# adaLN chunks of a diffusion trunk step: four column strips of the array instead of one, folded by the product that turns them

## The reference

```
mod = (silu(cond) @ w_ada + b_ada)          # cond: one row for context, one for latent; w_ada: 1024 x 6144
sh1, sc1, gt1, sh2, sc2, gt2 = split(mod, 6)
h = rms_norm(x, g_mix) * (1 + sc1) + sh1;  p = h @ w_in
# three mixers on p: attention (8 heads), chunked gated linear attention (GLA), RWKV-7, forward and backward
merged = sum over mixers of sigmoid(gate) * (mixer @ w_po)
x = x + gt1 * (merged @ w_out)
x = x + gt2 * ((silu(u) * v) @ w_ffn_out)   # (u, v) from (rms_norm(x, g_ffn) * (1 + sc2) + sh2) @ w_ffn_in
```

## Time and profile before

| what | value |
|---|---|
| median of three runs | 2113.26 us |
| the profiled execution: own time | 2109.75 us |
| the profiled execution: span | 2107.8 us |
| TensorE busy | 1912.7 us (91%) |
| DVE, ACT busy | 1011.0 us, 817.6 us |
| adaLN matmuls (L606), busy | 175.5 us |
| mean granted TensorE clock | 0.968 |

### The profile page before, as it was taken

One profiled execution on the slowest core, in us unless ns is written; L12 is line 12 of the kernel. 1 busy time (PEld: TensorE's weight loads), 2 busy tenths in 40 slices (PEclk: granted clock), 3 DMA queues, 4 the chain that ended last, 5 costly groups with the idle time before them and its releaser, 6 DMA issues.

```text
span 2107.8 us, 38529 instructions
## 1 busy us (share of the span) xinstructions
PE 1912.7 (91%) x16691; PEld 1552.8 (74%) x16691; DVE 1011.0 (48%) x1755; ACT 817.6 (39%) x1340; POOL 147.6 (7%) x325
## 2 busy tenths in 40 slices
PE   6899899986889898999989999999678989899998
PEld 3799455644566598999989975456356759899998
DVE  0326435856754354343333444177767445433432
ACT  2433545343433335333243345253534343533321
POOL 2000000005220000000000000000232200000000
PEclk9999999998999999999999999999889999999999
DMA  6533324220212443443433432333010034344342
GB/s 229 181 122 111 101 67 149 93 74 2 93 52 82 154 120 81 134 126 100 131 125 103 136 99 83 123 128 101 25 42 23 3 90 133 84 130 131 103 122 85
DMA packets 267934, 214.46 MB, mean 102 GB/s; under 512 B 7225, under 2 KB 259544, under 8 KB 267512
## 3 DMA queue, kind: packets, MB, share of 16 engines
q1 hardware_dynamic: 264816, 204.41, 31.5%
q0 software_dynamic: 2736, 7.54, 1.1%
q10 hardware_dynamic: 216, 0.06, 0.0%
HBM read 209.10 MB, written 2.88 MB: 101 GB/s over the span
## 4 chain that ended last, share of the span: by engine, by line
PE 76%; DVE 10%; ACT 9%; issue 3%; DMA 1%; PEldq 1%; ACTq 0%; PEld 0%; POOL 0%; DVEq 0%; SPq 0%; POOLq 0%
PE bank L555 11%; PE bank L557 11%; PE bank L556 11%; PE bank L611 9%; PE bank L606 7%; PE bank L1166 3%; PE bank L1167 3%; PE bank L1168 3%; PE bank L974 3%; PE bank L617 2%; PE bank L515 2%; PE bank L814 2%; ACT h L1348 1%; PE bank L916 1%; DVE scr_rounded L1782 1%
## 5 line engine op out<-in xcount | busy, mean ns | idle before, releaser
L557 PE MATMUL bank<-scr_rounded 128*128 128x384 f32 (+1 forms) x1312 | 444.1, 338 | 0.0
L555 PE MATMUL bank<-scr_rounded 128*128 128x384 f32 x672 | 232.5, 346 | 37.1 <-DVE scr_rounded L1787 35.6
L557 PEld LDWEIGHTS bank<-scr_rounded 128*128 128x128 f32 (+1 forms) x1312 | 249.7, 190 | 1.0
L611 PE MATMUL bank<-h,ring 128*128 128x384 f32 x640 | 233.8, 509 | 13.5 <-ACT gtmp L1331 8.0
L556 PE MATMUL bank<-scr_rounded 128*128 128x384 f32 x672 | 229.9, 342 | 0.0
L1782 DVE TENSOR_TENSOR scr_rounded<-ring,scr_rounded 128x2048 fp32r<-128x2048 f32 (+1 forms) x64 | 136.0, 2126 | 191.0 <-ACT scr_rounded L1339 190.2
L555 PE MATMUL bank<-scr_rounded,gate_rounded 128*128 128x384 f32 (+1 forms) x640 | 214.8, 336 | 4.4 <-DVE scr_rounded L1782 4.4
L556 PE MATMUL bank<-scr_rounded,gate_rounded 128*128 128x384 f32 (+1 forms) x640 | 214.4, 335 | 0.0
L611 PEld LDWEIGHTS bank<-h,ring 128*128 128x128 f32 x640 | 118.2, 194 | 96.0 <-issue 26.8
L606 PE MATMUL bank<-ring,scond 128*2 128x256 f32 x768 | 175.5, 381 | 9.0 <-DVEq L350 5.0
L1782 DVE TENSOR_TENSOR scr_rounded<-ring,gate_rounded 128x2048 fp32r<-128x2048 f32 (+3 forms) x64 | 130.1, 2033 | 106.1 <-ACT gate_rounded L1339 105.6
(11 more groups left out here) (383 smaller groups left out, 3236.5 us busy)
## 6 DMA issues: line engine op xcount, KB each, us to landing
ring<-in_w_in_dram SPq DMA_DIRECT2D x56, 1024.0 KB, 5.1
ring<-in_w_ada_dram SPq DMA_DIRECT2D x48, 1024.0 KB, 5.3
ring<-in_w_ffn_in_dram SPq DMA_DIRECT2D x88, 512.0 KB, 5.0
ring<-in_w_ffn_out_dram SPq DMA_DIRECT2D x32, 704.0 KB, 4.6
ring<-in_w_out_dram SPq DMA_DIRECT2D x8, 1024.0 KB, 5.2
ring<-in_w_po_a_dram SPq DMA_DIRECT2D x4, 1024.0 KB, 6.9
ring<-in_w_po_b_dram SPq DMA_DIRECT2D x4, 1024.0 KB, 5.9
ring<-in_w_po_c_dram SPq DMA_DIRECT2D x4, 1024.0 KB, 5.1
```

The costliest lines, as they stand in the source:

```text
L555: pe.matmul(o, w_hi[:, k, :], right[0][k], start=k == 0, stop=False)
L557: ins = pe.matmul(o, w_lo[:, k, :], right[0][k], start=False, stop=k == nk - 1)
L611: ins = pe.matmul(b[:, 0:T], w[:, k, 128 * (j % 2):128 * (j % 2) + 128], h[:, k, :], start=k == 0, stop=k == KD - 1)
```

## The change

The 8 matmuls of a chunk go to four column strips of the array: k = 0 to 3 open partitions 0, 32, 64 and 96 of the bank, k = 4 to 7 add to them. So there are four partial pairs of rows. ACT copies all 128 partitions of the bank. In place of the transposes two products with a constant `fold` (1 where the partition modulo 32 is the column) add the four and turn them. The fill banks are cleared once at the start, since unwritten partitions are now read. A chunk is one step of a fill and no longer two, so the numbers of steps are spread anew: both `fill(4)` at the start become `fill(2)`; in attention every third pair gets 3 steps; in GLA's loop steps alternate 1 and 2; layer 0's row of `FILLS` sums to 48 and no longer 56.

```
-        modrow = sb("modrow", [2, 2, 256])
+        modrow = sb("modrow", [128, 2, 256])
+    put("fold", p[:, None] % 32 == np.arange(2)[None, :])
...
-        FILLS = ((4, 6, 2, 1, 1, 1, 1, 0, 1, 1, 1, 2, 2, 2, 1, 1, 3, 2, 2, 1, 1, 3, 2, 2, 1, ...
+        FILLS = ((4, 6, 2, 1, 1, 1, 1, 0, 1, 1, 1, 1, 1, 2, 1, 1, 2, 2, 1, 1, 1, 2, 2, 1, 1, ...
...
                 for i in range(2):
-                    ins = turn(b[:, 2 * i:2 * i + 2], modrow[0:2, j % 2, 128 * i:128 * i + 128])
+                    ins = pe.matmul(b[:, 2 * i:2 * i + 2], modrow[:, j % 2, 128 * i:128 * i + 128], K("fold"), start=True, stop=True)
...
                         for k in range(KD):
-                            ins = pe.matmul(b[0:2, 0:256], scond[:, :, k], w[:, k, :], start=k == 0, stop=k == KD - 1)
-                            if k == 3:
-                                yield
+                            strip = 32 * (k % 4)
+                            ins = pe.matmul(b[strip:strip + 2, 0:256], scond[:, :, k], w[:, k, :], start=k < 4, stop=k >= 4)
...
-            fill(4)
+            pe.wait_ge(S["strips_clear"], 1)
+            fill(2)
...
-                    fill(2)
+                    fill(3 if pair % 3 == 0 else 2)
...
                 for n in range(2 * LEVELS):
-                    fill(2)
+                    fill(2 if n % 2 else 1)
...
-                        A(modrow[0:2, j % 2, :], bank(*t)[0:2, 0:256], ACT.Copy).then_inc(*empties(*t))
+                        A(modrow[:, j % 2, :], bank(*t)[:, 0:256], ACT.Copy).then_inc(*empties(*t))
...
+            dve.memset(banks[6][:, :], 0.0).then_inc(*step())
+            dve.memset(banks[7][:, :], 0.0).then_inc(*tells("strips_clear"))
```

More of the change, by code:

```diff
@@ L20 @@
 ROPE_THETA, GRID_W = 10000.0, 64
-_COLS = [("ident", 128), ("ones", 128), ("blocks", 128), ("eps", 4), ("dup", 256), ("duprot", 256), ("rot", 128),
+_COLS = [("ident", 128), ("ones", 128), ("blocks", 128), ("eps", 4), ("fold", 2), ("dup", 256), ("duprot", 256), ("rot", 128),
          ("cos", 256), ("sin", 256), ("upper", LEVELS * 128), ("lower", LEVELS * 128),
@@ L271, in step_kernel @@
         S = {n: sem(n) for n in (
-            "zeroed", "squares", "rstd", "normed",
+            "zeroed", "strips_clear", "squares", "rstd", "normed",
             "att_squares", "att_rstd", "att_normed", "att_keys", "att_queries", "att_max", "att_probs",
@@ L336, in counting @@
             return step, tells, empties, lambda: last, before
-        PER.update(zeroed=0, squares=8, rstd=2, padded=2, ffo_half=8, normed=16, h_hi=24, h_lo=24, src_hi=1, src_lo=1, mg_hi=8, mg_lo=8, ff_hi=NF, ff_lo=NF,
+        PER.update(zeroed=0, strips_clear=0, squares=8, rstd=2, padded=2, ffo_half=8, normed=16, h_hi=24, h_lo=24, src_hi=1, src_lo=1, mg_hi=8, mg_lo=8, ff_hi=NF, ff_lo=NF,
                    att_squares=1, att_rstd=5, att_normed=5, att_keys=1, att_queries=1, att_max=24, att_probs=24,
@@ L353, in barrier @@
                     eng.wait_ge(phase[other], l * NPHASE + k + 1)
-        FILLS = ((4, 6, 2, 1, 1, 1, 1, 0, 1, 1, 1, 2, 2, 2, 1, 1, 3, 2, 2, 1, 1, 3, 2, 2, 1, 1, 1, 1, 1, 1, 1, 2, 2, 2),
+        FILLS = ((4, 6, 2, 1, 1, 1, 1, 0, 1, 1, 1, 1, 1, 2, 1, 1, 2, 2, 1, 1, 1, 2, 2, 1, 1, 1, 1, 1, 1, 1, 1, 2, 1, 1),
                  (4, 6, 2, 1, 1, 1, 1, 0, 1, 1, 1, 1, 1, 1, 1, 1, 2, 1, 1, 1, 1, 2, 1, 1, 1, 1, 1, 1, 1, 1, 1, 1, 1, 1))
```

## The result

The changed kernel takes 2098.8 us (median of 4 runs, 2096.8 to 2104.0), the kernel before 2116.1 in the same session: a ratio of 0.9925, 95% interval 0.9907 to 0.9942. It is faster by 0.75%: the direction was forecast, the size was not. The forecast of 2040 was 59 us too low, and 2098.8 lies outside its range (2013 to 2067).

What follows compares the result with a forecast made beforehand. TensorE was taken to bound the kernel (76% of the chain). Gains of 15 (start) + 2 x 13 (attention) + 2 x 7.6 (GLA) + 15 (RWKV, layer 0) = 71 us gave 2038.5, stated as 2040; range 2013 to 2067.

Steps and rivals of the forecast that it cites:

- Chunk and fold: On TensorE, a chunk takes 0.97 us and its fold 0.35; together 1.32 instead of 3.75.
- Rivals B: Two strips run at a time, so a chunk is 0.87 us longer: 2061 us in all; chance 0.13.
- E (serial): Strips' records are issued one after another; nothing is saved and each fold adds 0.14 us: 2120 us; chance 0.04.
- the prediction's signs of being wrong: Wrong if a chunk takes 1.8 us or more, TensorE never waits for loads in attention, or GLA's loop still takes 64.
- The start: Up to the first projection: weight loads, not the row of chunks, end last; first projection at 49.5 us, gain 15.
- Attention: Each layer's attention takes 104 us, a gain of 13, with 7.2 us of new waits for gate weight loads.
- one late fold or so adds 1: In attention, besides the waits for gate loads, a late fold or so costs 1 us per layer.
- GLA: Each layer gains 7.6 us; DVE bounds the loop, which takes 57 us and ends at 421.3 instead of 428.9.
- Its first `gla_z` comes from ACT and DVE and does not move: In GLA, the first `gla_z`, made by ACT and DVE, keeps its old time, with the loop's blocks counted from 364.08.
- RWKV of layer 0: Its 8 chunks give a gain of 15 us (12.6 to 17.8), if the new 1.32 us are all exposed.
- So a chunk costs (28.3 - 5.2) / 8 = 2.9 to 3.5 of its 3.75: From the 28.3 us between RWKV's two layers, each chunk costs 2.9 to 3.5 of its 3.75 us.
- Rival C: Load waits at the start, in attention and in GLA exceed the count: gain 43 us, 2069 in all; chance 0.10.

Runs made afterwards that it cites:

- experiment 9: Only the first of the four strips multiplied (a quarter of each sum), against the kernel with strips and the old step counts (2075.5 us): 2077.9 us.
- experiment 7: 8 idle matmuls put into two TensorE waits (GLA's scaled keys, attention's late gate load), against the kernel with strips and the old step counts (2075.5 us): 2069.8 us.
- experiment 5: Changed kernel with three step numbers altered: attention's three steps every second pair, five steps ahead of GLA's scaled keys, GLA's loop counts swapped: 2079.6 us.
- experiment 4: Changed kernel with adaLN's weights not loaded but for one chunk; each chunk multiplies whatever weights its neighbour in the plan has in the ring: 2070.8 us.
- the kernel of 1: Strips and fold as in the changed kernel, but the step counts of before and a chunk in two steps again: 2075.5 us.
- experiment 3: Changed kernel with five steps instead of six ahead of the wait for GLA's scaled keys: 2109.2 us.
- Experiment 8: Each chunk's strips multiplied a second time into columns nobody reads, against the kernel with strips and the old step counts (2075.5 us): 2082.2 us.
- experiment 10: RWKV layer 0's 8 chunks moved to the end of GLA's plan, against strips with old step counts and reordered attention (2068.9 us): 2074.4 us.

## Why the prediction was wrong, step by step

**Chunk and fold: right.** 0.97 and 0.36 at the high clock. Rivals B (two strips at a time) and E (serial) are out by these rows and by experiment 9. None of the prediction's signs of being wrong came either: a chunk takes 1.05 at the high clock, attention waits 5.5 for loads, and GLA's loop takes 59.2 and 56.9 instead of 64. They watch the terms that were priced; the loss lay in what the sum took as unchanged.

**The start, 15 forecast, 9.9 measured.** The step that failed is the clock, which the sum put at its high level for everything behind the first two chunks; "the loads are late instead" holds only with it. In the changed kernel the start is as long without adaLN's loads (54.8), and what ends last is TensorE's own row of chunks, at the low clock. Here are a stretch of the changed kernel, and then of the kernel of experiment 7, whose start has the same chunks at the same places; the ACT rows are the split of the first projection weights.

```profile
27.31 1.89 PE L608 MATMUL bank<-ring,scond 128*2 128x256 f32 x16 [2.46 <-ACT modrow L1319]
29.12 1.01 PE L591 MATMUL bank<-cst,modrow 128*128 128x2 f32 x4
30.00 7.02 PE L541 MATMUL bank<-mg,cst 128*128 128x384 f32 x16
...
45.27 1.89 PE L608 MATMUL bank<-ring,scond 128*2 128x256 f32 x16
...
47.56 1.90 ACT L1340 ACTIVATE scr_rounded<-ring 128x2048 fp32r<-128x2048 f32 x1
```

The kernel of experiment 7:

```profile
26.63 1.05 PE L611 MATMUL bank<-ring,scond 128*2 128x256 f32 x16 [2.46 <-ACT modrow L1331]
27.60 0.61 PE L591 MATMUL bank<-cst,modrow 128*128 128x2 f32 x4
28.07 5.41 PE L541 MATMUL bank<-mg,cst 128*128 128x384 f32 x16
...
42.70 1.91 ACT L1352 ACTIVATE scr_rounded<-ring 128x2048 fp32r<-128x2048 f32 x1 [1.40 <-DMA ring<-in_w_in_dram]
...
49.93 0.66 PE L556 MATMUL bank<-scr_rounded 128*128 128x384 f32 x1 [7.91 <-DVE scr_rounded L1800]
```

After the same wait of 2.46 us the one is at the low clock (granted 0.50 from 27 to 31) and the other is not (1.00 from 26.6 to 42). In the latter the split waits for its load and starts at 42.70, where 42.3 was forecast, and the first projection comes at 49.93, where 49.5 was forecast. So the mechanism of the start holds at the high clock, and 5 us of the miss were the clock. Experiment 7's edit does not touch the start. The kernels of this text whose start has these same chunks and loads reach the first projection between 49.9 and 54.8, and why one start keeps the high clock and another does not stays open.

**Attention, 13 forecast, 3.9 measured in each layer.** The waits for loads came nearly as counted (5.5 against 7.2). What failed is "one late fold or so adds 1". I followed only the ring's slots and not the two fill banks: at three places the new counts put a chunk right behind a gate's last step and a fold, one bank is the fold's, and the other is the gate's until ACT's sigmoid has emptied it. That is 6.2 us in each layer, and 3.4 to 3.5 more by the low clock on unchanged work. Experiments 5 and 4 take the two waits away one at a time, and attention falls to 101.6 to 104.5 and to 103.1.

**GLA, 7.6 forecast, 4.5 lost in layer 0 and 2.4 won in layer 1.** The loop was nearly right: with the old spread it ends after 58 us (57 forecast), and DVE holds it. What failed is "Its first `gla_z` comes from ACT and DVE and does not move". In the changed kernel the first block product came 40.3 us after the stage's first matmul in layer 0, before 32.2 (364.12 less 331.93). Ahead of it TensorE waits for DVE's scaled keys, before too (the prediction calls it a wait for ACT). The transposes behind that wait, before:

```profile
357.44 1.09 PE L515 MATMUL bank<-cst,scr 128*128 128x128 f32 x8 [2.42 <-DVE scr L1965]
```

The setup after the change:

```profile
318.08 3.58 PE L759 MATMUL bank<-arena,lora 32*128 32x384 f32 x8 [0.75 <-DVEq L351]
321.58 2.93 PE L769 MATMUL bank<-arena 64*128 64x128 f32 x24
324.44 6.58 PE L617 MATMUL bank<-arena,ring 128*128 128x384 f32 x16
...
340.50 1.91 PE L608 MATMUL bank<-ring,scond 128*2 128x256 f32 x32 [0.42 <-DVE mg L1773]
345.27 0.58 PE L591 MATMUL bank<-cst,modrow 128*128 128x2 f32 x4 [2.86 <-ACT modrow L1319]
349.57 1.97 PE L516 MATMUL bank<-cst,scr 128*128 128x128 f32 x8 [3.72 <-DVE scr L1968]
351.47 3.24 PE L801 MATMUL bank<-gate,scr 128*64 128x128 f32 x32
```

Low clock at the top (the kernel of 1 takes 2.84, 1.61 and 5.43 for the first three), a second chunk and a fold that waits for ACT's copy where six steps used to hold one chunk, and low clock again on the products whose results DVE waits for. DVE starts late because TensorE does. The transposes stand 31.5 us after the stage's first matmul here, 25.5 before, and 28.7 in experiment 3, which has the same low clock at the top but neither the second chunk nor the fold there: about 3 us are the low clock, 3 the chunk and fold, and 2 more come behind them. Layer 1 runs the same instructions; its first block product comes after 38.1 us and its loop takes 56.9, at a mean clock of 0.94 instead of 0.90, so it is not the steps that part the two layers.

**RWKV of layer 0, 15 forecast, 1 measured.** What failed is "So a chunk costs (28.3 - 5.2) / 8 = 2.9 to 3.5 of its 3.75". The difference between the layers was a price of having chunks there, not of their length. Their own busy time fell by 16.6 as counted, 9.0 came back in unchanged work at a clock of 0.90 instead of 0.94, and 6.6 as idle time. Experiment 8 adds 7.0 us to those chunks and the stage moves by 3, within its scatter; experiment 10 takes them out and it falls by 28. Even the 1 us is not firm: the kernels of 3 and 5 run the same instructions in this stage and take 286.4 and 287.4.

**RWKV of layer 1**, which the sum took as fixed, lost 3.0 with the same instructions; the other ten kernels that run them lost between 0.6 and 6.0. Its cause stays open: no experiment was made on it.

The sum failed on two things, then. I priced moved steps by TensorE's time and the ring alone; experiment 1 puts that at 23 us. And I carried over durations from stages where TensorE was busy 92 to 94% of the time at a clock of 0.99 into stages where it is busy 82 to 83%; with RWKV of layer 0, unchanged work took 29 us more (18 with the old spread). Rival C had the sign (larger waits) but only for loads. The Trainium skill tells of a kernel whose work between waits for loads was shorter than the waits and which fell back to the low clock at every tile (TensorE: Matmul & The Clock Gate, "HAM oscillation — how this bites in real kernels"). The rows of experiment 7 agree: behind a wait of 3.69 us for a load the gate records took 7.69, and 5.43 when the wait was filled. I should have made a rival of it.

## What to carry to other kernels

When a change takes work from an engine that was nearly always busy, do not carry its old durations over: price the unchanged work at both clocks, and allow for waits that cost more than their length (in attention here 1.4 to 1.9 times). When steps are moved, follow every resource that a step holds (here two PSUM banks that ACT and DVE empty, beside the ring's slots), at each place where two steps become neighbours. A difference between two stages, one with some work and one without, is the price of having that work; only changing its length shows the price of its length.

## What was unexpected of the hardware

- Three further column strips cost nothing: 4 records in 1.03 us, 16 in 1.04.
- The same wait of 2.46 us on the same chunks was followed by the low clock in one kernel (1.89 us for a chunk) and by the high one in another (1.05).
- 41.8 us of extra matmuls cost 6.8 us, and the mean granted clock over the profiled span rose from 0.951 to 0.963.
